# Four feed-forwards on one core: the order of the weight queue's loads, and one addition moved ahead

## The chip, the cores and the metric

The kernel runs on one core of a Trainium2 chip. The metric is the device time of one execution in microseconds, and lower is better. The kernel before takes 2634.15 us, the median of three runs (2631.6 to 2635.01).

## What is computed

Two transformer blocks of two layers each, for 512 tokens of width 1024, all in float32. Each of the four layers ends in a feed-forward, and only these four are touched here:

```
hn = rms_norm(h, gain)                                   # [512, 1024]
h = h + jnp.square(jax.nn.relu(hn @ w1)) @ w2            # w1 [1024, 4096], w2 [4096, 1024]
```

In the second block the norm has a shift and a scale, and the product with `w2` is multiplied by a gate before it is added. The mixers between the feed-forwards (a spatial gate, two chunked recurrences, two attentions) stay as they are.

## The kernel before

Everything is held transposed: 128 features on the partitions, 512 tokens along the free axis. A float32 product is made of three matmuls on values that are cut into a high and a low part (`hi*hi + hi*lo + lo*hi`), so every weight has to be cut before use: ACT writes the high part (`w_hi`), DVE or POOL writes the low part (`w_lo = raw - hi`).

**Loads.** SP issues all weight loads, in one written order (`mlp_stream`, lines 504 to 546). A load of `w1` is a *chunk* (line 509): 128 columns, 512 KB. A load of `w2` is a *half chunk* (line 514): 512 rows by 256 columns, also 512 KB; two of them feed the four products of one step. Each load waits, on SP, for its buffer to be read for the last time. SP handles its list strictly in order, so a load that waits holds back all that stand behind it. In the first three feed-forwards ACT also issues loads of its own (`ada_load_one`, line 563, 512 KB each), up to three per step, for a modulation vector that is summed beside the feed-forward.

**The steps.** A feed-forward begins with six chunks in the plain form and the first four products with `w2` (step 0). Then come the steps `hp` = 1 to 13, and last steps 14 and 15, which have products with `w2` only. Each step 1 to 13 does two things on TensorE (`mlp_tensor`):

- the *pair*: two new chunks of the hidden layer, by seven products P1 to P7 on quarters (Strassen's scheme in Winograd's form, line 1363 and the two after it), instead of eight;
- four products with `w2`, g0 to g3 (line 1398 and the next), for hidden values made earlier; each is added to `h` by DVE (`add`, line 1704).

TensorE's order within a step is P1, P2, g0, P4, P5, P6, g1, P7, g2, P3, g3. P3 adds to a bank that DVE must have read first (`last_quarters`, line 1681).

**The pair's two chunks.** For the step `hp + 1`, the first chunk is needed for its P1 and P2 cuts. The second is needed inside step `hp`: DVE makes the sums S3 and S1 from both chunks (`sums_13(ahead)`, lines 1658 and 1659) right behind `add(hp, 1)`, and ACT makes the high part of P4 from it (line 1489). DVE's list in a step is:

```
mid_low, [ada], low P6, first_quarter, low P7, sum_4 (S4), add g0, [ada], low P3, low P1', [ada], low P2',
add g1, S3', S1', last_quarters, low P4', scaled, add g2, low P5', second_quarter, scaled, S2', mid_low, add g3
```

A prime marks work for the step ahead. The two `scaled` operations are there in the first two feed-forwards only (line 1692), and `[ada]` in the first three. `last_quarters` stands behind S3' and S1' in DVE's list, and TensorE's P3 waits for it.

**What SP waits for.** The second chunk of step `hp + 1` waits for S4 of step `hp` (line 1669). The two half chunks wait for POOL's low cuts of g1 and of g3 of step `hp` (line 654). The first chunk of step `hp + 2` waits for the low cut of P3 of step `hp`. POOL's cut of g3 follows ACT's high part of g3, which stands in ACT's list right behind the high part of P3, which is made from the sum S4.

**The first steps.** In step 0, DVE's list ends: low parts of the turned activations (`t_low`), `add(0, 1)`, `t_low(3)`, `std_rest(5)` (which waits for ACT), `sums_13(1)`, `add(0, 2)`, and so on. TensorE's g0 of step 1 waits for `add(0, 2)`, since it writes the same bank.

Here is how the pair loop of SP reads:

```
for which in range(2):
    ... wait ...
    chunk(...)
for half in range(2):
    sp.wait_ge(*g_cut(i, hp - 1, 2 * half + 1))
    g_chunk(hp, half)
```

Of the kernel before, what the change touches and what calls it, by code (L numbers as in the profile page):

```python
# [102 lines left out]
def program(nc: bass.Bass, dram, out, upto="end"):  # L103
    rows, col, n_tables = vector_rows()
    ctx = ExitStack()
    with ctx:
# [55 lines left out]
        def ready(q, j):  # L162
            return w_ready, 4 * q + j + 1
# [235 lines left out]
        def out_quad(i):  # L399
            return quads[mlp_out[i]] + 1  # L400

        def place(hp, what):

            if hp == 0:
                return 12 + int(what[1])
            if hp >= 14:
                return 160 + 4 * (hp - 14) + int(what[1])
            return 16 + 11 * (hp - 1) + PAIR.index(what)

        def spent(i, n):  # L410
            return ml_spent, N_HALVES * i + n + 1

        def std_cut(i, c, part="lo"):
            return ml_pool, 76 * i + 2 * c + (2 if part == "lo" else 1)

        def g_cut(i, hp, c):
            return ml_pool, 76 * i + 12 + 4 * hp + c + 1
# [9 lines left out]
        def low_cut(i, hp, what):  # L427
            return ml_low, 143 * i + 11 * (hp - 1) + PAIR_LOWS.index(what) + 1
# [19 lines left out]
        def std_acted(i, what, n):  # L448
            return std_act, 12 * i + 2 * n + (2 if what == "hi" else 1)

        def t_at(i, what):
            return t_dve, 20 * i + T_DVE.index(what) + 1

        def t_acted(i, what, n):
            return t_act, (12 * i if i < 2 else 24 + 4 * (i - 2)) + n + 1 + (8 if what == "hi" and i < 2 else 0)
# [8 lines left out]
        def raw_slot(s):  # L464
            return w_raw[:, s, :, :] if s < 4 else raw_extra
# [4 lines left out]
        def pair_load(hp, which):  # L470
            n = 2 * (hp - 1) + which
            s = RING[n % 3]
            return s, n // 3 + (0 if s == 4 else 2)

        def g_load(hp, half):
            if hp < 14:
                return 2 + half, 1 + hp
            return (half, 11) if hp == 14 else (2 + half, 15)

        def land(s):  # L480
            return w_load[s] if s < 4 else extra_load
# [22 lines left out]
        def mlp_stream(sp, i):  # L504

            w1, w2 = mlp_w[i]

            def chunk(s, c):
                sp.dma_start(raw_slot(s), w1[:, c * P:(c + 1) * P].rearrange("(k p) n -> p k n", p=P)).then_inc(land(s), 16)

            def g_chunk(hp, half):
                s, at = g_load(hp, half)[0], hp // 2 * 512
                n = 4 * (hp % 2) + 2 * half
                sp.dma_start(raw_slot(s).rearrange("p (k n) c -> p k (n c)", n=2),
                             w2[at:at + 512, n * P:(n + 2) * P].rearrange("(k p) m -> p k m", p=P)).then_inc(land(s), 16)

            for c in range(4):
                sp.wait_ge(*ready(out_quad(i), c))
                chunk(c, c)
            for which in range(2):  # L520
                sp.wait_ge(*std_cut(i, which))
                chunk(which, 4 + which)
            for half in range(2):
                sp.wait_ge(*std_cut(i, 2 + half))
                g_chunk(0, half)
            for hp in range(1, 14):
                for which in range(2):
                    n = 2 * (hp - 1) + which
                    if n < 2:
                        sp.wait_ge(*std_cut(i, 4 + n))  # L530
                    elif n == 2:
                        sp.wait_ge(*t_at(i, "lo3"))
                    elif n % 2:
                        sp.wait_ge(*low_cut(i, 1 + (n - 3) // 2, "S4"))
                    else:
                        sp.wait_ge(*low_cut(i, 1 + (n - 3) // 2, "P3"))
                    chunk(pair_load(hp, which)[0], 4 * (hp // 2 + 1) + 2 * (hp % 2) + which)
                for half in range(2):
                    sp.wait_ge(*g_cut(i, hp - 1, 2 * half + 1))
                    g_chunk(hp, half)  # L540
            for half in range(2):
                sp.wait_ge(*low_cut(i, 13, "P3" if half else "S4"))
                g_chunk(14, half)
            for half in range(2):
                sp.wait_ge(*g_cut(i, 13, 2 * half + 1))
                g_chunk(15, half)
# [648 lines left out]
        def gate_col(block2_layer, half, n):  # L1195
            if block2_layer is None:
                return 1.0
            c = 48 * block2_layer + 24 * half + 16 + n
            return mod[:, c:c + 1]
# [112 lines left out]
        def g_bank(i, hp, c):  # L1312
            if hp >= 14 and i == 3:
                return ps[0] if c % 2 else ps[3]
            return ps[3 + c % 2]

        def t_pair(p):
            return t_tiles[:, 2 * p:2 * p + 2, :].rearrange("p a t -> p (a t)")
# [274 lines left out]
        def mlp_vector(v, i, layer2, norm_before, next_norm):  # L1593
# [17 lines left out]
            def std_rest(n):  # L1611
                v.wait_ge(*std_acted(i, "hi", n))
                nc.vector.tensor_tensor(m_lo[:, n, :], tt[:, n % 2, :], m_hi[:, n, :].bitcast(F32), ALU.subtract
                                        ).then_inc(std_dve, 1)
# [27 lines left out]
            def t_low(p):  # L1642
                v.wait_ge(*t_acted(i, "hi", p))
                nc.vector.tensor_tensor(xt_lo[:, p, :], t_pair(p), xt_hi[:, p, :].bitcast(F32), ALU.subtract
                                        ).then_inc(t_dve, 1)

            def low(hp, what):
                n = place(hp, what)
                v.wait_ge(*high_cut(i, hp, what))
                nc.vector.tensor_tensor(half_slot(w_lo, n), pair_block(hp, what), half_slot(w_hi, n).bitcast(F32),  # L1650
                                        ALU.subtract).then_inc(ml_low, 1)

            def sums_13(hp):
                a11, _ = quarters_of(hp, 0)
                a21, a22 = quarters_of(hp, 1)
                v.wait_ge(*ml_loaded(i, *pair_load(hp, 0)))
                v.wait_ge(*ml_loaded(i, *pair_load(hp, 1)))
                nc.vector.tensor_tensor(s3_tile, a11, a21, ALU.subtract).then_inc(ml_low, 1)
                nc.vector.tensor_tensor(a21, a21, a22, ALU.add).then_inc(ml_low, 1)
# [41 lines left out]
            def add(hp, c):  # L1701
                n = 4 * (hp % 2) + c
                v.wait_ge(*spent(i, place(hp, f"g{c}")))
                nc.vector.scalar_tensor_tensor(out=h[:, n, :], in0=g_bank(i, hp, c)[:, :], scalar=gate_col(layer2, 1, n),  # L1704
                                               in1=h[:, n, :], op0=ALU.mult, op1=ALU.add).then_inc(ml_added, 1)
# [25 lines left out]
            t_low(2)  # L1731
            add(0, 1)
            t_low(3)
            std_rest(5)
            sums_13(1)
            add(0, 2)
            low(1, "P4")
            low(1, "P5")
            sum_2(1)
# [1936 lines left out]
        def mlp(i, norm_before, next_norm, layer2=None):  # L3676
            return (lambda e: mlp_tensor(e, i, norm_before), lambda e: mlp_scalar(e, i, norm_before, next_norm),
                    lambda e: mlp_vector(e, i, layer2, norm_before, next_norm))
# [175 lines left out]
```

## Time and profile before

| | us |
|---|---|
| Median of three runs | 2634.15 |
| The profiled execution | 2635.26 |
| Its span (first to last instruction) | 2633.5 |
| TensorE busy | 2583.0 (98%) |
| VectorE busy | 1911.9 (73%) |
| ScalarE busy | 1297.3 (49%) |
| GpSimd busy | 1345.1 (51%) |
| Longest group of waits of TensorE in the feed-forwards | 6.6 |

The four feed-forwards lie at about 330 to 676, 1000 to 1330, 1640 to 2005 and 2280 to 2630 us. A busy share is an average over stages. What a reordering is worth in the feed-forwards is read from TensorE's waits there and from how long before its need each load lands.

### The profile page before, as it was taken

Reading aid. Unit: us, or ns where it says so; the run is one execution under the profiler, and the core shown is the slowest. Engines: PE = TensorE matmul, PEld = TensorE weight load, DVE = VectorE, ACT = ScalarE, POOL = GpSimd, SP = SyncE. Lnnn points to the kernel's source line nnn. Section 1 sums busy time; section 2 is a strip of 40 time slices with the busy share of each in tenths; the row PEclk is TensorE's granted clock in tenths of the full one; section 3 lists DMA queues with packets and bytes.
Section 4 is the critical chain, followed back from the end, with each engine's and each line's share of the span. In section 5 each row is a group of like instructions: output and inputs, shape, how many; then the busy total and the mean of one; then the engine's idle time right before and its main releaser. Section 6 shows DMA issues by size and latency. Waiting matters only on the chain.

```text
span 2633.5 us, 39135 instructions
## 1 busy us (share of the span) xinstructions
PE 2583.0 (98%) x14420; PEld 2132.7 (81%) x14420; DVE 1911.9 (73%) x2755; ACT 1297.3 (49%) x2291; POOL 1345.1 (51%) x1720
## 2 busy tenths in 40 slices
PE   9999999999999999999999999999999999999999
PEld 7777788888867778888887887788887666789998
DVE  4766578997677767999854577888875776786664
ACT  4455344444356644444432354455554776455553
POOL 5543543334866665433476866543336655643333
PEclk9999999999999999999999999999999999999999
DMA  5211135554321223555332321255543211233332
GB/s 145 68 48 42 54 123 160 161 160 137 103 72 56 65 64 110 180 166 161 120 120 72 88 65 58 88 170 170 167 138 92 62 59 56 64 97 97 97 97 88
DMA packets 359671, 272.77 MB, mean 104 GB/s; under 512 B 9786, under 2 KB 346052, under 8 KB 359492
## 3 DMA queue, kind: packets, MB, share of 16 engines
q1 hardware_dynamic: 343618, 216.68, 27.8%
q10 hardware_dynamic: 15874, 53.67, 6.1%
q8 instruction: 116, 1.90, 0.3%
q14 instruction: 63, 0.52, 0.1%
HBM read 268.22 MB, written 2.10 MB: 103 GB/s over the span
## 4 chain that ended last, share of the span: by engine, by line
PE 75%; DVE 8%; POOL 7%; issue 5%; ACT 3%; DMA 1%; ACTq 0%; POOLq 0%; DVEq 0%; SPq 0%
PE pair L1401 8%; PE pair L1398 8%; PE pair L1402 8%; POOL w_lo L585 5%; PE ps L1363 4%; PE ps L1366 4%; PE ps L1365 4%; PE pair L1363 3%; PE pair L1366 3%; PE pair L1365 3%; PE ps L675 3%; PE ps L2641 2%; PE ps L677 2%; PE ps L676 2%; POOL w_hi L578 2%
## 5 line engine op out<-in xcount | busy, mean ns | idle before, releaser
L654 POOL TENSOR_TENSOR w_lo<-w_raw,w_hi 128x256 fp32r<-128x256 f32 x512 | 486.5, 972 | 758.4 <-ACT w_hi L1480 758.3
L585 POOL TENSOR_TENSOR w_lo<-w_raw,w_hi 128x256 fp32r<-128x256 f32 x588 | 498.2, 877 | 12.3
L1398 PE MATMUL pair<-m_hi,w_hi 128*128 128x512 f32 x1008 | 394.8, 392 | 4.6 <-DVE h L1704 4.6
L1401 PE MATMUL pair<-m_lo,w_hi 128*128 128x512 f32 x1008 | 395.5, 392 | 0.0
L1402 PE MATMUL pair<-m_hi,w_lo 128*128 128x512 f32 x1008 | 394.4, 391 | 0.0
L591 POOL TENSOR_TENSOR slot_mark<-slot_mark 128x1 f32<-128x1 f32 x168 | 44.2, 263 | 484.3 <-PE ps L677 218.4
L1398 PEld LDWEIGHTS pair<-m_hi,w_hi 128*128 128x128 f32 x1008 | 189.8, 188 | 40.8 <-issue 5.2
L675 PE MATMUL ps<-x_hi,w_hi 128*128 128x512 f32 x528 | 218.1, 413 | 4.5 <-DVE x_lo L1170 2.5
L1402 PEld LDWEIGHTS pair<-m_hi,w_lo 128*128 128x128 f32 x1008 | 189.3, 188 | 40.9
L1489 ACT ACTIVATE w_hi<-w_raw 128x512 fp32r<-128x512 f32 x216 | 135.3, 628 | 176.8 <-DVE w_raw L1669 97.1
L1480 ACT ACTIVATE w_hi<-w_raw 128x512 fp32r<-128x512 f32 x256 | 157.6, 624 | 125.9 <-DMA w_raw<-in_w_mlp_dram 42.5
L1401 PEld LDWEIGHTS pair<-m_lo,w_hi 128*128 128x128 f32 x1008 | 189.7, 188 | 33.5
L677 PE MATMUL ps<-x_hi,w_lo 128*128 128x512 f32 x528 | 206.8, 392 | 0.0
L676 PE MATMUL ps<-x_lo,w_hi 128*128 128x512 f32 x528 | 206.2, 391 | 0.0
L578 POOL TENSOR_SCALAR w_hi<-w_raw 128x512 fp32r<-128x512 f32 x294 | 202.3, 705 | 0.0
L1650 DVE TENSOR_TENSOR w_lo<-w_raw,w_hi 128x512 fp32r<-128x512 f32 x216 | 177.8, 835 | 10.6 <-ACT w_hi L1489 10.6
L1704 DVE SCALAR_TENSOR_TENSOR h<-pair,mod,h 128x512 f32<-128x512 f32 x124 | 93.0, 750 | 121.5 <-PE pair L1402 121.4
L2641 PE MATMUL ps<-x_hi,w_hi 128*128 128x512 f32 x336 | 139.6, 415 | 1.5
L1495 ACT ACTIVATE rb<-ps 128x256 f32<-128x256 f32 x156 | 59.8, 383 | 155.5 <-PE ps L1366 155.4
L2643 PE MATMUL ps<-x_hi,w_lo 128*128 128x512 f32 x336 | 131.7, 392 | 0.0
L2642 PE MATMUL ps<-x_lo,w_hi 128*128 128x512 f32 x336 | 131.6, 392 | 0.0
L1704 DVE SCALAR_TENSOR_TENSOR h<-pair,h 128x512 f32<-128x512 f32 x128 | 87.8, 686 | 60.3 <-PE pair L1402 60.0
(552 smaller groups left out, 7056.6 us busy)
## 6 DMA issues: line engine op xcount, KB each, us to landing
w_raw<-in_w_mlp_dram SPq DMA_DIRECT2D x112, 512.0 KB, 5.3
w_raw<-in_mlp_w_dram SPq DMA_DIRECT2D x112, 512.0 KB, 5.2
arena<-in_ada_w_dram ACTq DMA_DIRECT2D x96, 512.0 KB, 4.6
w_raw<-in_w_in_ab_dram SPq DMA_DIRECT2D x28, 512.0 KB, 3.8
w_raw<-in_w_qkv_o_dram SPq DMA_DIRECT2D x24, 512.0 KB, 3.7
w_raw<-in_w_qkv_dram SPq DMA_DIRECT2D x24, 512.0 KB, 3.8
w_raw<-in_w_in_e_dram SPq DMA_DIRECT2D x23, 512.0 KB, 4.1
arena<-in_w_mlp_dram SPq DMA_DIRECT2D x16, 512.0 KB, 5.5
```

The source lines that it names most:

```text
L578: last = nc.gpsimd.tensor_scalar(w_hi[:, j, k, :], w_raw[:, j, k, :], 1.0, 1.0, ALU.mult, ALU.mult)
L585: last = nc.gpsimd.tensor_tensor(w_lo[:, j, k, :], w_raw[:, j, k, :], w_hi[:, j, k, :].bitcast(F32), ALU.subtract)
L654: last = nc.gpsimd.tensor_tensor(half_slot(w_lo, n)[:, k, :], g_half(hp, c)[:, k, :], half_slot(w_hi, n)[:, k, :].bitcast(F32), ALU.subtract)
L675: nc.tensor.matmul(bank[:, :], w_hi[:, j, k, :], hi[:, k, :], start=(k == 0), stop=False)
L676: nc.tensor.matmul(bank[:, :], w_hi[:, j, k, :], lo[:, k, :], start=False, stop=False)
L677: last = nc.tensor.matmul(bank[:, :], w_lo[:, j, k, :], hi[:, k, :], start=False, stop=(k == ND - 1))
L1363: nc.tensor.matmul(out, hi[:, t, :], b_hi[:, t, :], start=(start and t == 0), stop=False, skip_group_check=True)
L1365: nc.tensor.matmul(out, hi[:, t, :], b_lo[:, t, :], start=False, stop=False, skip_group_check=True)
L1398: first = nc.tensor.matmul(bank[:, :], hi[:, t, :], m_hi[:, m, :], start=(t == 0), stop=False)
L1401: nc.tensor.matmul(bank[:, :], hi[:, t, :], m_lo[:, m, :], start=False, stop=False)
L1402: last = nc.tensor.matmul(bank[:, :], lo[:, t, :], m_hi[:, m, :], start=False, stop=(t == 2))
L2641: nc.tensor.matmul(ps[0][:, :], w_hi[:, j, k, :], hi[:, k, :], start=(k == 0), stop=False)
```

## The change

Two edits. In SP's list, for the steps 2 to 13, both half chunks now stand between the pair's first and second chunk. Step 1 is as before. In DVE's list of step 0, `add(0, 2)` goes ahead of `std_rest(5)` and `sums_13(1)`. No instruction is added or removed, no wait is changed, and buffers are the same.

```diff
@@ mlp_stream
                     chunk(pair_load(hp, which)[0], 4 * (hp // 2 + 1) + 2 * (hp % 2) + which)
-                for half in range(2):
-                    sp.wait_ge(*g_cut(i, hp - 1, 2 * half + 1))
-                    g_chunk(hp, half)
+                    if which == (1 if hp == 1 else 0):
+                        for half in range(2):
+                            sp.wait_ge(*g_cut(i, hp - 1, 2 * half + 1))
+                            g_chunk(hp, half)
@@ mlp_vector
             add(0, 1)
             t_low(3)
+            add(0, 2)
             std_rest(5)
             sums_13(1)
-            add(0, 2)
             low(1, "P4")
```

In SP's list of the first feed-forward, the loads of steps 1 to 4 stood like this before (a row with `128x8x128` is a chunk, one with `128x4x256` a half chunk, `x2` means two in a row; the third buffer for chunks is called `arena`):

```order
L509 DMA w_raw<-in_w_mlp_dram 128x8x128 x2
L514 DMA w_raw<-in_w_mlp_dram 128x4x256 x2
L509 DMA arena<-in_w_mlp_dram 128x8x128
L509 DMA w_raw<-in_w_mlp_dram 128x8x128
L514 DMA w_raw<-in_w_mlp_dram 128x4x256 x2
L509 DMA w_raw<-in_w_mlp_dram 128x8x128
L509 DMA arena<-in_w_mlp_dram 128x8x128
L514 DMA w_raw<-in_w_mlp_dram 128x4x256 x2
```

and now:

```order
L509 DMA w_raw<-in_w_mlp_dram 128x8x128 x2
L514 DMA w_raw<-in_w_mlp_dram 128x4x256 x2
L509 DMA arena<-in_w_mlp_dram 128x8x128
L514 DMA w_raw<-in_w_mlp_dram 128x4x256 x2
L509 DMA w_raw<-in_w_mlp_dram 128x8x128 x2
L514 DMA w_raw<-in_w_mlp_dram 128x4x256 x2
L509 DMA arena<-in_w_mlp_dram 128x8x128
L509 DMA w_raw<-in_w_mlp_dram 128x8x128
```

The second chunk of each step from 2 on now stands behind the step's two half chunks and right ahead of the next step's first chunk.

In DVE's list of the first feed-forward, the end of step 0 before, from `add(0, 1)` on:

```order
L1704 SCALAR_TENSOR_TENSOR h<-pair,h 128x512
L1644 TENSOR_TENSOR xt_lo<-arena,xt_hi 128x1024
L1613 TENSOR_TENSOR m_lo<-tt,m_hi 128x512
L1658 TENSOR_TENSOR tt<-w_raw 128x512
L1659 TENSOR_TENSOR w_raw<-w_raw 128x4x128
L1704 SCALAR_TENSOR_TENSOR h<-pair,h 128x512
L1650 TENSOR_TENSOR w_lo<-w_raw,w_hi 128x512 x2
```

and now (lines behind the first edit count one higher):

```order
L1705 SCALAR_TENSOR_TENSOR h<-pair,h 128x512
L1645 TENSOR_TENSOR xt_lo<-arena,xt_hi 128x1024
L1705 SCALAR_TENSOR_TENSOR h<-pair,h 128x512
L1614 TENSOR_TENSOR m_lo<-tt,m_hi 128x512
L1659 TENSOR_TENSOR tt<-w_raw 128x512
L1660 TENSOR_TENSOR w_raw<-w_raw 128x4x128
L1651 TENSOR_TENSOR w_lo<-w_raw,w_hi 128x512 x2
```

The second addition moved three instructions ahead: it stands before the low part of the last plain chunk and the first pair's two sums.

## Rows read from the trace of the kernel before

**Rows 1.** The page, busy time of each engine over the span.
```profile
PE 2583.0 (98%) x14420; PEld 2132.7 (81%) x14420; DVE 1911.9 (73%) x2755; ACT 1297.3 (49%) x2291; POOL 1345.1 (51%) x1720
```

**Rows 2.** TensorE's waits: engine, tile, line, for whom: us in total, times, longest.
```profile
PE pair L1363 <- DVE sq L1681: 6.6, 4, 3.0
PE pair L1398 <- DVE h L1704: 4.6, 6, 1.3
```

**Rows 3.** SP's issues in step 5, first feed-forward: start, us taken, line.
```profile
471.72 0.37 SPq L514 DMA_DIRECT2D w_raw<-in_w_mlp_dram  x1
472.13 0.51 SPq L509 DMA_DIRECT2D w_raw<-in_w_mlp_dram  x1
```

**Rows 4.** Loads issued at 352.7, 468.6, 470.7, 472.1, 380.8 us: KB, us to landing.
```profile
w_raw<-in_w_mlp_dram SPq DMA_DIRECT2D x1, 512.0 KB, 3.6
...
w_raw<-in_w_mlp_dram SPq DMA_DIRECT2D x1, 512.0 KB, 5.5
...
arena<-in_ada_w_dram ACTq DMA_DIRECT2D x1, 512.0 KB, 4.6
...
w_raw<-in_w_mlp_dram SPq DMA_DIRECT2D x1, 512.0 KB, 6.5
...
w_raw<-in_w_mlp_dram SPq DMA_DIRECT2D x1, 512.0 KB, 7.9
```

**Rows 5.** DVE in steps 5 and 6, first feed-forward: start, us, line.
```profile
467.48 0.68 DVE L1669 TENSOR_TENSOR w_raw<-arena,w_raw 128x512 f32<-128x512 f32 x1
...
475.48 0.68 DVE L1658 TENSOR_TENSOR tt<-w_raw,arena 128x512 f32<-128x512 f32 x1
476.08 1.23 DVE L1659 TENSOR_TENSOR arena<-arena 128x512 f32<-128x512 f32 x1
477.23 0.68 DVE L1681 TENSOR_TENSOR sq<-pair,rb 128x512 f32<-128x512 f32 x1
...
488.58 0.68 DVE L1669 TENSOR_TENSOR arena<-w_raw,arena 128x512 f32<-128x512 f32 x1
```

**Rows 6.** P3's first matmul in step 5, feed-forwards one, three and four.
```profile
478.88 0.28 PE L1363 MATMUL pair<-x_hi,w_hi 128*128 128x256 f32 x1
...
1807.90 0.28 PE L1363 MATMUL pair<-x_hi,w_hi 128*128 128x256 f32 x1
...
2429.90 0.28 PE L1363 MATMUL pair<-x_hi,w_hi 128*128 128x256 f32 x1
```

**Rows 7.** SP issuing the later half chunk, step 5, feed-forwards three and four.
```profile
1800.53 0.37 SPq L514 DMA_DIRECT2D w_raw<-in_mlp_w_dram  x1
...
2421.47 0.37 SPq L514 DMA_DIRECT2D w_raw<-in_mlp_w_dram  x1
```

**Rows 8.** P3's first matmul in steps 1 and 12, feed-forwards one and two.
```profile
390.99 0.52 PE L1363 MATMUL pair<-x_hi,w_hi 128*128 128x256 f32 x1 [3.02 <-DVE sq L1681]
...
628.06 0.28 PE L1363 MATMUL pair<-x_hi,w_hi 128*128 128x256 f32 x1
...
1056.50 0.39 PE L1363 MATMUL pair<-x_hi,w_hi 128*128 128x256 f32 x1 [1.30 <-DVE sq L1681]
...
1290.93 0.28 PE L1363 MATMUL pair<-x_hi,w_hi 128*128 128x256 f32 x1
```

**Rows 9.** SP issuing the later half chunk in step 1, feed-forwards one and two.
```profile
383.95 0.37 SPq L514 DMA_DIRECT2D w_raw<-in_w_mlp_dram  x1
...
1051.17 0.37 SPq L514 DMA_DIRECT2D w_raw<-in_w_mlp_dram  x1
```

**Rows 10.** Busy time, instructions, granted clock, DMA share, GB/s behind the longest wait.
```profile
391.00:394.50 3.50, 3.50 (x14) 3.31 (x15) 2.91 (x6) 1.81 (x3) 0.00 (x0) 0.51 0.35 129
```

**Rows 11.** ACT in step 1 of the first feed-forward.
```profile
388.73 0.63 ACT L1480 ACTIVATE w_hi<-w_raw 128x512 fp32r<-128x512 f32 x1 [5.76 <-DMA w_raw<-in_w_mlp_dram]
```

**Rows 12.** `add(0, 2)` and the g0 that waits for it, second feed-forward.
```profile
1040.10 0.68 DVE L1704 SCALAR_TENSOR_TENSOR h<-pair,h 128x512 f32<-128x512 f32 x1
...
1040.93 0.47 PE L1398 MATMUL pair<-m_hi,w_hi 128*128 128x512 f32 x1 [0.89 <-DVE h L1704]
```

## The prediction

> **What bounds the kernel now.** I read the page first: TensorE is busy for 98% of the span, every other engine for 73% or less [rows 1]. So there is almost nothing to win, and the question is what lies idle in the feed-forwards and how close the other waits are to showing. The waits of TensorE say what is idle. Those that this change can touch are 6.6 us in four waits at P3, which waits for DVE's `last_quarters`, and 4.6 us in six waits of products with `w2` for an addition to `h` [rows 2]. That is 0.4% of the time. The longest is 3.0 us in step 1 of the first feed-forward, and behind it the granted clock was 0.51, its lower level of 1.2 GHz, for most of 3.5 us [rows 8, 10]. ACT had waited there 5.76 us for the step's early half chunk, which took 7.9 us to land behind the second chunk and two loads of ACT [rows 11, 4]. This is what the new order would help.
>
> Then I read the order of time of SP, DVE and TensorE inside one later step, since steps 2 to 13 repeat with a period of 21.10 us (S4 starts at 467.48 and at 488.58) [rows 5]. There TensorE waits for nothing. What counts is the slack. In step 5 of the first feed-forward, S3' starts at 475.48, S1' at 476.08, `last_quarters` runs from 477.23 to 477.91, and P3 starts at 478.88 [rows 5, 6]. P3 could have borne 0.97 us less the handover, which is 0.06 us.
>
> **The queue edit.** It moves no work, it moves one landing. Until now SP issued the second chunk of the next step as soon as S4 ended, at 468.16 (467.48 + 0.68). Now it stands behind the later half chunk, which waits for POOL's cut of g3 and was issued at 471.72; the next entry of the list followed 0.41 us later, at 472.13 [rows 3]. So the second chunk goes out at 472.13 instead of about 468.2, 3.9 us later.
>
> *How long it then takes to land (D).* No row shows this chunk in this place. The nearest are: 3.6 us for a load with nothing in flight; 5.5 us for one issued 0.41 us behind another; 6.5 us for the one at 472.13, which had the older loads and one of ACT's in front (ACT's own took 4.6) [rows 4]. The earlier half chunk will be out of the way by then, so I take 5.5, from the row with the same neighbour in front, and keep 3.6 and 6.5 as ends; 7.9 is the worst row.
>
> The Trainium skill (DMA: Bandwidth & Descriptors, section Anatomy of one DMA) gives 2.0 us plus the bytes over 436 GB/s for one transfer, though for the gpsimd path. By that page 512 KB would be an estimated 3.2 us alone and 4.0 us behind another one. No row here is so short.
>
> *What hangs on it.* S3' and S1' read the second chunk, and `last_quarters` stands behind them. S3' start to the end of `last_quarters` is 2.43 us now; S1' took 1.23 us where S3', of the same shape, took 0.68, and POOL's cut of g0' beside it now comes earlier (its half chunk is no longer late), so I take 2.43 − 0.55 = 1.9. From the later half chunk's issue to P3 it is then 0.41 + D + 1.9 + 0.1 for two handovers, **7.9 us with D = 5.5**. The room is 478.88 − 471.72 = 7.16 us in the first two feed-forwards, 1807.90 − 1800.53 = 7.37 in the third, 2429.90 − 2421.47 = 8.43 in the fourth [rows 3, 6, 7]. So P3 comes 0.75 us late, 0.5 us late, and in time. ACT's P4' and the cut behind it wait for the same landing, but need only about 1.0 us before `last_quarters`, less than S3' and S1', so they are hidden.
>
> *The circle.* Lateness feeds itself. Late S3' shifts all of DVE's list behind it up to S4 of the next step; S4 releases ACT's P3 and g3 and POOL's cut, that releases the later half chunk, and that the next second chunk. From S3' (475.48) to the end of S4 (489.26) are 13.78 us, with nearly no gap in the first two feed-forwards; less 0.55 for S1' and some 0.1 of gaps, 13.1. From the end of S4 (468.16) to the half chunk's issue (471.72), 3.56. With 0.41, D = 5.5 and 0.05 of handover the circle is **22.6 us**. A step took (1290.93 − 1056.50) / 11 = 21.31 us on the mean [rows 8]. DVE had idle time before; waiting for the load uses it up. So the steps of the first two feed-forwards get 1.3 us longer each. In the third there are no two `scaled` (0.6 us each) and the circle is near 21.8, so P3's own lateness counts, 0.5 to 0.75: I take 0.6. In the fourth DVE has no `[ada]` either, and the circle is hidden.
>
> **The addition.** `add(0, 2)` has 0.6 us of DVE (0.68 with overlapped ends), and stands in front of S3' and S1' of step 1 no more. TensorE's g0 had waited 0.89 us for it in the second feed-forward [rows 12]. `std_rest(5)` waits for ACT anyway, so the addition is free ahead of it. TensorE's own gain at g0 is given back, since P3 of step 1 was late in three feed-forwards; what stays is DVE's 0.6 us. Once per feed-forward, all queues behind it 0.6 us earlier.
>
> **Sum, against the profiled execution (2635.3 us).**
>
> - *First steps.* First feed-forward: 383.95 − 0.6 + 7.9 = 391.25 against 390.99, +0.3 [rows 8, 9]. Second: 1051.17 − 0.6 + 7.9 = 1058.5 against 1056.50, +2.0. Third: as the second, +2.0, and since the whole wait is then over 3 us, the lower clock behind it as in the first: 3.5 us at 0.51 cost half, +1.8 [rows 10]. In the second DVE's circle hides that. Fourth: +0.5, P3 had no wait there before.
> - *Later steps, eleven from P3 of step 1 to P3 of step 12.* First: 11 × 22.6 = 248.6 against 628.06 − 390.99 = 237.1, +11.5. Second: 248.6 − 234.4 = +14.2. Third: 11 × 0.6 = +6.6. Fourth: 0.
>
> Together 11.8 + 16.2 + 10.4 + 0.5 = **+38.9 us**, so 2674.2; the median of the runs shown was 1.1 us under the profiled execution, so I predict **2673 us**, 1.5% slower. What a measurement of this kernel can tell from no change is about 0.2%, 5.3 us.
>
> **Rivals.**
>
> - *Hidden.* If the second chunk lands within 4.4 us of its issue in the first two feed-forwards (22.6 − 21.31 = 1.3 less than 5.5 would be 4.2, P3's own room gives 4.75), nothing shows in the later steps. For it: ACT's load falls behind it (ACT issues the third one after P4', which now waits) and the half chunks leave its way. Against: 5.5 us in a row with just one load in front. The first steps then give −0.8 in the first, about +0.8 in each of the next two: near 2635. By the page's estimate of 4.0 us this is what would come out. Chance 0.08.
> - *Faster.* The place is step 1 of the first feed-forward: with the half chunk no longer late and a landing of 3.6 us, P3 starts at 389.3, 1.7 us earlier; a wait as short as the 1.3 us of the second feed-forward left the clock up, so the 1.8 us go too, and about 1.1 us of the other three waits of [rows 2], first line. With the addition's 0.6 us twice that is 5.8 us, about 2628. It decides from D = 3.7 downwards. Chance 0.07.
> - *Heavier.* The three loads now go out in one burst with ACT's beside them. With D = 6.5 the circle is 23.6: 11 more us in each of the first three and P3 0.5 us late in each step of the fourth: +38.9 + 33 + 5.5 + 4 = +81, about 2716. For it: 6.5 and 7.9 in rows 4. Chance of more than 2712: 0.10.
> - That the edit does nothing can be left out: eleven issues per feed-forward are moved for certain, and the later half chunk's wait is a real one.
>
> **Chances.** The forecast's mechanism, with D from 4.7 to 6.4, gets 0.75 and spans 2642 (at 4.7: circle 21.8, +5 and +7 in the first two feed-forwards, nothing in the later steps of the others) to 2712. The range 2642 to 2712 leaves out the hidden and faster cases and the worst of the heavier. Faster by over 0.2%: 0.07; within: 0.08; slower: 0.85.
>
> **What would show it.** In the profile after: a second chunk issued about 0.4 us behind the later half chunk; DVE idle 2 us before S3' (L1659 there), with a DMA as the releaser; TensorE's wait at P3 for `last_quarters` in nearly every step, some 30 of them over 0.5 us; steps of about 22.6 us in the first two feed-forwards, 21.9 in the third, 21.1 in the fourth; g0 of step 1 with no wait for an addition. Wrong would be: a landing under 4.7 us with no wait at P3 (hidden), steps of equal length in all four feed-forwards (then no circle through DVE), or the fourth as slow as the others (then it is the burst, not DVE's list).

## The result, and the profile after

The changed kernel takes **2754.6 us** (median of 4 runs, 2752.4 to 2762.5) against 2632.9 us before (median of 4 runs on the same chip). The ratio is 1.0466, with an interval of 1.0452 to 1.0480: 122 us slower. Predicted were 2673 us and at most 2712.

The page of the kernel after, busy times. The third figure of an engine's group is its number of instructions.

```profile
PE 2618.8 (95%) x14420; PEld 2152.8 (78%) x14420; DVE 1910.0 (69%) x2755; ACT 1286.1 (47%) x2291; POOL 1358.9 (49%) x1720
```

The work is the same, but TensorE is busy for 35.8 us more than in [rows 1], its weight loads for 20 and GpSimd for 14. A large part of TensorE's is work done at the lower clock: in run 6 below, with 56 us less of that clock, it is busy for 24 us less. The span grew by 119 us, from 2633.5 to 2752.6. The summary of its chain of waits says who holds the end:

```profile
PE 58%; DVE 15%; DMA 9%; POOL 7%; issue 6%; ACT 4%; ACTq 0%; DVEq 0%; POOLq 0%
```

The same line of the kernel before, in which DMA has 1% and TensorE 75%:

```profile
PE 75%; DVE 8%; POOL 7%; issue 5%; ACT 3%; DMA 1%; ACTq 0%; POOLq 0%; DVEq 0%; SPq 0%
```

TensorE's waits after, which answer to [rows 2]:

```profile
PE pair L1364 <- DVE sq L1682: 90.5, 37, 6.6
PE pair L1399 <- DVE h L1705: 2.4, 4, 1.0
```

P3 waits 37 times for `last_quarters`, 90.5 us in all, where there were four waits and 6.6 us. All but two of the 37 are in the first three feed-forwards. The addition's waits went from 4.6 to 2.4 us. DVE in turn waits for the second chunk before S3' (three of its four lines with a DMA as the releaser; with the fourth, 18.7 us, they are 48 waits of 3.0 us on the mean):

```profile
DVE tt L1659 <- DMA w_raw<-in_w_mlp_dram: 62.3, 16, 5.3
DVE tt L1659 <- DMA w_raw<-in_mlp_w_dram: 33.8, 16, 4.2
DVE tt L1659 <- DMA arena<-in_w_mlp_dram: 27.2, 8, 4.8
```

One turn of the circle, in order of time, steps 4 and 5 of the second feed-forward. DVE first (start, us taken, line, and in brackets how long it was idle and what ended that):

```profile
1171.73 0.69 DVE L1659 TENSOR_TENSOR tt<-arena,w_raw 128x512 f32<-128x512 f32 x1 [3.78 <-DMA w_raw<-in_w_mlp_dram]
1172.34 0.69 DVE L1660 TENSOR_TENSOR w_raw<-w_raw 128x512 f32<-128x512 f32 x1
1172.94 0.69 DVE L1682 TENSOR_TENSOR sq<-pair,rb 128x512 f32<-128x512 f32 x1
...
1184.00 0.68 DVE L1670 TENSOR_TENSOR w_raw<-arena,w_raw 128x512 f32<-128x512 f32 x1
...
1196.52 0.69 DVE L1659 TENSOR_TENSOR tt<-w_raw,arena 128x512 f32<-128x512 f32 x1 [4.82 <-DMA arena<-in_w_mlp_dram]
```

SP's queue in the same stretch, and what it says of the landing of the load at 1188.65 (KB, us from issue to landing):

```profile
1188.24 0.37 SPq L514 DMA_DIRECT2D w_raw<-in_w_mlp_dram  x1
1188.65 0.51 SPq L509 DMA_DIRECT2D arena<-in_w_mlp_dram  x1
...
arena<-in_w_mlp_dram SPq DMA_DIRECT2D x1, 512.0 KB, 7.8
```

S3' starts at 1171.73, S4 ends at 1184.68 (12.95 us), the later half chunk is issued at 1188.24 (3.56), the second chunk 0.41 behind it, it lands 7.8 us later, and the next S3' starts at 1196.52: 24.8 us for a step that took 21.3. S3' start to the end of `last_quarters` is 1173.63 − 1171.73 = 1.90 us, and P3 follows at 1173.68:

```profile
1173.68 0.38 PE L1364 MATMUL pair<-x_hi,w_hi 128*128 128x256 f32 x1 [2.25 <-DVE sq L1682]
```

P3's first matmul after, in steps 1 and 12 of the four feed-forwards in turn (the first and second pairs answer to [rows 8]):

```profile
395.09 0.58 PE L1364 MATMUL pair<-x_hi,w_hi 128*128 128x256 f32 x1 [5.86 <-DVE sq L1682]
...
666.41 0.39 PE L1364 MATMUL pair<-x_hi,w_hi 128*128 128x256 f32 x1 [0.62 <-DVE sq L1682]
...
1098.70 0.58 PE L1364 MATMUL pair<-x_hi,w_hi 128*128 128x256 f32 x1 [6.03 <-DVE sq L1682]
...
1369.31 0.39 PE L1364 MATMUL pair<-x_hi,w_hi 128*128 128x256 f32 x1 [0.57 <-DVE sq L1682]
...
1805.66 0.58 PE L1364 MATMUL pair<-x_hi,w_hi 128*128 128x256 f32 x1 [6.55 <-DVE sq L1682]
...
2073.90 0.37 PE L1364 MATMUL pair<-x_hi,w_hi 128*128 128x256 f32 x1
...
2463.03 0.39 PE L1364 MATMUL pair<-x_hi,w_hi 128*128 128x256 f32 x1
...
2696.66 0.28 PE L1364 MATMUL pair<-x_hi,w_hi 128*128 128x256 f32 x1
```

Over eleven steps that is 271.3, 270.6, 268.2 and 233.6 us, where before it was 237.1, 234.4, 234.4 (1722.7 to 1957.1) and 232.0 (2345.5 to 2577.5). So **the later steps cost +34.2, +36.2, +33.8 and +1.6 us, 106 of the 119**, and a step is 24.7, 24.6, 24.4 and 21.2 us long. The first steps (from P1's first matmul to P3's) cost +2.7, +3.6, +4.2 and +0.3; the remaining 2.5 us are elsewhere.

And the landing time in place. The burst of step 4, first feed-forward: a load of ACT at 460.12, the later half chunk at 461.03, the second chunk at 461.44, the next first chunk at 461.99 (KB, us to landing, in this order). Then a half chunk and a second chunk at 2518.0 and 2518.4 in the fourth feed-forward, which has no load of ACT. Last, the second chunk of step 13 in the first feed-forward, issued at 659.40, which has none beside it either:

```profile
arena<-in_ada_w_dram ACTq DMA_DIRECT2D x1, 512.0 KB, 4.1
...
w_raw<-in_w_mlp_dram SPq DMA_DIRECT2D x1, 512.0 KB, 6.4
...
w_raw<-in_w_mlp_dram SPq DMA_DIRECT2D x1, 512.0 KB, 7.6
...
w_raw<-in_w_mlp_dram SPq DMA_DIRECT2D x1, 512.0 KB, 8.6
...
w_raw<-in_mlp_w_dram SPq DMA_DIRECT2D x1, 512.0 KB, 3.7
...
w_raw<-in_mlp_w_dram SPq DMA_DIRECT2D x1, 512.0 KB, 5.1
...
w_raw<-in_w_mlp_dram SPq DMA_DIRECT2D x1, 512.0 KB, 5.0
```

The means in the trace after (us; D is the second chunk's issue to landing), with those before in brackets. The first two columns are over the loads of steps 3 to 13, the last three over those of steps 2 to 13:

| feed-forward | D | later half chunk to landing | S3' start to S4 end | S4 end to half chunk's issue | that issue to S3' |
|---|---|---|---|---|---|
| 1 | 6.9 (4.4) | 5.6 (6.0) | 13.4 (14.1) | 3.8 (3.7) | 7.5 (3.7) |
| 2 | 6.9 (4.4) | 5.6 (5.6) | 13.3 (13.8) | 3.8 (3.7) | 7.5 (3.6) |
| 3 | 7.1 (4.5) | 5.5 (5.6) | 12.8 (13.3) | 4.0 (4.0) | 7.7 (3.9) |
| 4 | 5.4 (4.4) | 3.8 (4.9) | 12.4 (13.1) | 2.9 (2.9) | 5.8 (5.0) |

In the first three rows the last three columns add up to the measured step within 0.1 us (24.7, 24.6, 24.4): the circle closes. In the fourth row they make 21.1 and little waits. In the first three feed-forwards D depends on ACT: in the 33 steps 2 to 12 a load of ACT was issued 0.6 to 1.8 us ahead of the later half chunk, and D is 7.2 us on the mean; in the three steps 13 there is none, and D is 4.9. The granted clock was at about half (1.2 GHz) for 6.8 us of the span before and for 75.4 us, in 18 stretches, of the span after.

### The profile page after: what moved, and what is told of

Same layout as the page of the kernel before. It is cut to its first block, busy times and chain, and to the rows that moved or that the text cites. A ratio compares the mean times of both kernels' runs of the same rounds, so it can differ in the third digit from the quotient of the medians.

```text
span 2752.6 us, 39135 instructions
## 1 busy us (share of the span) xinstructions
PE 2618.8 (95%) x14420; PEld 2152.8 (78%) x14420; DVE 1910.0 (69%) x2755; ACT 1286.1 (47%) x2291; POOL 1358.9 (49%) x1720
## 4 chain that ended last, share of the span: by engine, by line
PE 58%; DVE 15%; DMA 9%; POOL 7%; issue 6%; ACT 4%; ACTq 0%; DVEq 0%; POOLq 0%
PE pair L1399 5%; PE pair L1402 5%; PE pair L1403 5%; POOL w_lo L586 5%; DMA w_raw<-in_w_mlp_dram 4%; DVE w_lo L1651 3%; PE ps L676 2%; DMA w_raw<-in_mlp_w_dram 2%; PE ps L2642 2%; PE ps L678 2%; PE ps L677 2%; PE ps L1364 2%; POOL w_hi L579 2%; PE pair L1364 2%; PE ps L1367 2%
## 5 line engine op out<-in xcount | busy, mean ns | idle before, releaser
L655 POOL TENSOR_TENSOR w_lo<-w_raw,w_hi 128x256 fp32r<-128x256 f32 x512 | 499.4, 998 | 862.3 <-ACT w_hi L1481 862.2
L586 POOL TENSOR_TENSOR w_lo<-w_raw,w_hi 128x256 fp32r<-128x256 f32 x588 | 497.9, 877 | 12.3
L1399 PE MATMUL pair<-m_hi,w_hi 128*128 128x512 f32 x1008 | 401.1, 398 | 2.4 <-DVE h L1705 2.4
L1364 PE MATMUL pair<-x_hi,w_hi 128*128 128x256 f32 x208 | 68.8, 331 | 90.6 <-DVE sq L1682 90.5
L1490 ACT ACTIVATE w_hi<-arena 128x512 fp32r<-128x512 f32 x96 | 60.0, 628 | 160.3 <-DVE arena L1670 49.0
```

Of the source, the lines that this page charges most:

```text
L586: last = nc.gpsimd.tensor_tensor(w_lo[:, j, k, :], w_raw[:, j, k, :], w_hi[:, j, k, :].bitcast(F32), ALU.subtract)
L655: last = nc.gpsimd.tensor_tensor(half_slot(w_lo, n)[:, k, :], g_half(hp, c)[:, k, :], half_slot(w_hi, n)[:, k, :].bitcast(F32), ALU.subtract)
L1399: first = nc.tensor.matmul(bank[:, :], hi[:, t, :], m_hi[:, m, :], start=(t == 0), stop=False)
L1490: nc.scalar.activation(half_slot(w_hi, n), pair_block(hp, what), ACT.Copy).then_inc(ml_hi, 1)
```

## The experiments

My theory after the result: the mechanism is the predicted one (late second chunk, circle through DVE's list and SP's queue), and D was mis-sized. Rivals for the size: the lower clock behind P3's waits, the bandwidth taken by the first chunk behind, or something in the addition. The kernel before, beside which they ran on the same chip, had medians of 2632.2 us (1 to 4), 2634.0 (5, 6, 7 and 11) and 2632.2 (8, 9, 10 and 12); the ratios are to these runs. They are formed from all runs and differ from the quotient of two medians by up to 0.0007.

**1, 2. Each part alone.** The first is the kernel before with the addition's line moved; the second is the changed kernel with the line put back, so only SP's order is changed:

```diff
             t_low(3)
+            add(0, 2)
             std_rest(5)
             sums_13(1)
-            add(0, 2)
```
(the second kernel has this piece reversed, against the changed kernel).

> Only the addition to h is moved ahead; SP's list is as before. If the whole slowdown is the queue's (my theory), this is 0.5 to 3 us faster than before: TensorE's wait of 0.9 us at g0 of step 1 in the second and of 1.3 us in the third feed-forward goes, and part of it is given back at P3. If the moved addition carries part of the slowdown, it is more than 5 us slower than before.

Measured: 2631.2 us, ratio 0.9996 (0.9987 to 1.0005). That lies in the range I gave, but it is not to be told from nothing. The trace shows what it does, TensorE's waits of this kernel:

```profile
PE pair L1363 <- DVE sq L1681: 5.6, 3, 2.1
PE pair L1398 <- DVE h L1704: 2.4, 4, 1.0
```

About 1.0 us less at P3 and 2.2 less at the additions, in a kernel whose runs differ by more.

> Only SP's list is changed. Theory: all of the +122 us, 2754 to 2757 us. Rival (the two edits hurt only together): under 2740 us.

Measured: 2758.9 us, 1.0481 (1.0465 to 1.0497), 2 us above the range of my theory and far from the rival's. **The queue's order carries all of the loss.**

**3. One half chunk between the chunks.** SP's order in a step is first chunk, early half chunk, second chunk, later half chunk; the addition stays ahead.

```diff
-                    if which == (1 if hp == 1 else 0):
-                        for half in range(2):
+                    if hp == 1 and which == 1 or hp > 1:
+                        for half in range(2) if hp == 1 else [which]:
                             sp.wait_ge(*g_cut(i, hp - 1, 2 * half + 1))
                             g_chunk(hp, half)
```

> SP's list of steps 2 to 13 is first chunk, early half chunk, second chunk, later half chunk, and the addition is ahead. The second chunk no longer stands behind POOL's cut of g3, so by my theory it goes out right behind S4 again, about 5.4 us into a step, lands near 9.5, and the slowdown is gone: 2624 to 2632 us, with the wait of 3 us at P3 in step 1 of the first feed-forward shorter, since ACT has its half chunk early. Rival (an early half chunk in itself disturbs the loads, or the split of the pair does): over 2660 us.

Measured: 2630.5 us, 0.9997 (0.9988 to 1.0006), as expected. The second chunk is out early again and D is 4.1 us. So it is the later half chunk, which waits for POOL's cut of g3, that the second chunk must not stand behind. The early one ahead of it costs nothing, and brings nothing that shows either: P3 still waits in three of the first steps.

```profile
PE pair L1364 <- DVE sq L1682: 5.9, 3, 2.3
```

**4. Take P3 off the late chunk, keep the circle.** The changed kernel with `last_quarters` ahead of `sums_13` in DVE's list, and ACT's snap P7 ahead of the cut P4'. P3 then needs nothing of the second chunk, but S4 still stands behind S3'.

```diff
                 add(hp, 1)
+                last_quarters(hp)
                 if hp < 13:
                     sums_13(ahead)
-                last_quarters(hp)
@@ on ACT
                 g_high(ahead, 0)
+                snap(hp, "P7", snap_v)
                 if hp < 13:
                     high(ahead, "P4")
                 ada_ahead(2)
-                snap(hp, "P7", snap_v)
```

> The changed kernel, with DVE's last_quarters ahead of S3' and S1' and ACT's snapshot of P7 ahead of the high part of P4', so that P3 does not wait for the second chunk. If the slowdown is P3's wait alone (the order of DVE's list), 2625 to 2645 us. If it is the circle (S3' late, DVE's list late up to S4, the later half chunk and the next second chunk late), the circle with the measured landing of 7 us is 12.5 + 3.6 + 0.4 + 7.0 + 0.1 = 23.6 us against 21.3, and the first three feed-forwards keep steps of 23 to 24 us: 2690 to 2720 us.

Measured: 2688.7 us, 1.0215 (1.0199 to 1.0231), at the lower end of what the circle would make (2690 to 2720) and far from the 2625 to 2645 of the other case. P3's own waits shrink to 13 us, the half clock to 3.4 us, and yet the kernel is 56 us slower than before. TensorE now waits for low parts that DVE makes late:

```profile
PE pair L1399 <- DVE m_lo L1699: 23.7, 29, 2.3
PE pair L1364 <- DVE sq L1682: 13.0, 22, 1.1
PE ps L1364 <- DVE w_lo L1651: 11.7, 9, 2.1
```

Steps (from P3 of step 1 to P3 of step 12, by eleven, as above) are 23.7, 23.9, 22.3 and 21.1 us. In the first feed-forward S3' to S4 is 12.3, then 3.7 and 7.4: 23.4, which again adds up to nearly the whole step, with D still at 6.8. **The circle is there with TensorE's wait at P3 taken out of it.** It also shows how much of a turn was TensorE's. S3' to S4's end fell from 13.4 to 12.3 us in the first feed-forward and from 12.8 to 10.8 in the third. Of either, 0.6 us is `last_quarters` itself, which stood in this stretch and now runs ahead of S3', while DVE waits for the load. The rest is mostly waits for TensorE: in this stretch DVE was idle for 0.5 and 1.6 us a turn in the changed kernel, each time for a product, and in run 4 for nothing in the first feed-forward and for 0.9 us, for ACT, in the third. Ahead of S4 in DVE's list stand `second_quarter`, which waits for P3, and `add(hp, 3)`, which waits for g3 behind it. P3's wait, the lower clock and this 0.6 us together are worth 66 us, and the other 56 are there without them.

**5. As late, but first in the burst.** One line holds the second chunk until POOL's cut of g3; it then goes out ahead of the later half chunk (the order is that of 3).

```diff
                         sp.wait_ge(*low_cut(i, 1 + (n - 3) // 2, "S4"))
+                        sp.wait_ge(*g_cut(i, hp - 1, 3))
```

> The order of the run before (early half chunk, second chunk, later half chunk), but the second chunk also waits for POOL's cut of g3, so it goes out as late as in the changed kernel, only in the later half chunk's place, 0.41 us earlier and first in the burst. Circle theory: it lands in the 5.6 us that the later half chunk took there, so the circle is 13.2 + 3.8 + 5.7 = 22.7 us in the first two feed-forwards, P3 late by 0.3 us in the third, nothing in the fourth: 2655 to 2675 us, some 85 us below the changed kernel for 1.7 us of earlier landing. Rival (cost follows from the late issue, whatever the landing): 2730 us or more.

Measured: 2671.8 us, 1.0150 (1.0133 to 1.0167), in the range of the circle theory and far from the rival's. D is 5.8, 5.8, 5.5 and 4.4 us. So with nothing of SP's queue right in front it is still 5.5 to 5.8 in the first three feed-forwards, and in the fourth, where ACT loads nothing, 4.4. The circle in the first: 12.9 + 4.2 + 5.5 = 22.6, with steps of 22.6 and 22.5 in the first two. One place nearer to the front, and 0.41 us less of issue, are worth 83 us.

**6. ACT's load out of the burst.** In the changed kernel ACT issues the second of its three loads of a step behind P4', with the third, instead of 0.6 to 1.8 us ahead of the later half chunk.

```diff
                     high(ahead, "P2")
-                ada_ahead(1)
                 snap(hp, "P6", snap_q)
                 g_high(ahead, 0)
                 if hp < 13:
                     high(ahead, "P4")
+                ada_ahead(1)
                 ada_ahead(2)
```

> The changed kernel, with ACT's second load of a step issued behind the high part of P4', so that none of ACT's loads is in flight when the later half chunk and the second chunk go out. If ACT's load is why the second chunk takes 6.9 to 7.1 us in the first three feed-forwards and 5.4 in the fourth, it takes 5.3 to 5.8 now, and the circle is 1.3 us shorter over 33 steps: 2700 to 2715 us. If the burst of SP's own three loads is the reason, the landing and the time stay: 2745 us or more.

Measured: **2672.2 us**, 1.0146 (1.0130 to 1.0162). That is 82 us less than the changed kernel, and 28 us below the range that I expected here. D came down as the theory said, but a step got 2.1 to 2.3 us shorter and not the 1.3 expected, over 36 steps and not 33. The time is nearly the one predicted for the changed kernel, since its steps are nearly those forecast there; in part that is luck, D being 0.3 us under the 5.5 taken and the wait for POOL's cut 0.2 over. D is 5.2, 5.2, 5.3 and 5.4 us: all four feed-forwards alike. One second chunk of the first feed-forward (issued at 473.71 us; KB, us to landing):

```profile
arena<-in_w_mlp_dram SPq DMA_DIRECT2D x1, 512.0 KB, 5.4
```

TensorE's waits at P3 fall to a third, with hardly fewer of them, and the half clock to 20 us:

```profile
PE pair L1364 <- DVE sq L1682: 32.8, 31, 4.5
```

The steps are 22.6, 22.5, 22.0 and 21.3. Over twelve steps and the first three feed-forwards that is (2.1 + 2.1 + 2.3) × 12 = 78 us less than in the changed kernel, so the steps hold nearly all of the 82. The later half chunk, next behind ACT's load before, took 3.7 us instead of 5.6.

**7. The first chunk held back.** In the changed kernel SP waits for the second chunk to have landed before it issues the next first chunk, so nothing is behind it in its queue.

```diff
                         sp.wait_ge(*low_cut(i, 1 + (n - 3) // 2, "P3"))
+                        sp.wait_ge(*ml_loaded(i, *pair_load(hp - 1, 1)))
```

> The changed kernel, with the next step's first chunk held on SP until the second chunk has landed, so that only two of SP's loads are in the burst. If the load behind it takes bandwidth from the second chunk, that one lands 0.5 to 1.5 us sooner and the time is 2700 to 2735 us. If what is behind in SP's own queue does not matter: within 6 us of the changed kernel.

Measured: 2730.8 us, 1.0370 (1.0354 to 1.0387), 24 us less than the changed kernel. The time lies in the range of the first case, but the landing that was to bring it does not: D hardly moved, 6.8, 6.9, 6.7 and 5.1 us against 6.9, 6.9, 7.1 and 5.4. That is 0.1, 0.1 and 0.4 us in twelve steps each, 7 us in all; the half clock was 61 us instead of 75. The span of the profiled execution was 2739 us, only 13 us under the changed kernel's, and its waits at P3 were 85.3 us in 37 times, close to the 90.5 above. **What stands behind the second chunk in its queue is not what makes D long.** Which of the small gains make up the 24 us stays open.

**8. Filler for the clock.** Six matmuls more in each of steps 1 to 12 of the first three feed-forwards, from TensorE, into a bank that nobody reads, ahead of P3's wait and behind one for ACT's cut of P3; what the kernel computes is unchanged.

```diff
                 g_product(hp, 2)
+                if i < 3 and hp < 13:
+                    pe.wait_ge(*low_cut(i, hp, "P3"))
+                    for _ in range(6):
+                        nc.tensor.matmul(ps[5][:, :], half_slot(w_hi, place(hp, "P3"))[:, 0, :], x_hi[:, 0, :],
+                                         start=True, stop=True)
                 pe.wait_ge(*pair_out(i, hp, "C2"))
```

> The changed kernel, and in steps 1 to 12 of the first three feed-forwards six more matmuls of 512 columns on TensorE ahead of P3's wait, into a bank that nobody reads (1.4 us of work inside a wait of 2.5 us on the mean; they change no result). They add 216 matmuls and shorten the idle time, so the lower clock should stay away. If the lower clock costs what 68 us at half speed lose (34 us), 2715 to 2725 us. If most of it is hidden behind DVE's circle in the first two feed-forwards, 2730 to 2745 us. If it costs nothing, 2750 to 2760 us, or more by what the filler delays in steps with a shorter wait.

Measured: 2746.9 us, 1.0440 (1.0420 to 1.0459). The time lies between two of my cases. The half clock fell from 75 to 40 us, and P3's waits from 90.5 to 50.4 us:

```profile
PE pair L1364 <- DVE sq L1687: 50.4, 31, 5.1
```

Yet the kernel gained only 8 us (7 by the ratios, whose intervals leave about 1 to 13 open), and the steps are still 24.8, 24.3 and 24.0 us. D was 7.3, 7.0 and 7.0 us, so 0.4 longer in the first feed-forward, which takes some 5 us of the gain away. **The lower clock is not the larger part of the loss.** A reason that fits, though no run shows it apart: TensorE runs slow while the circle, which doesn't wait for it most of the time, sets the end. By this run 36 us less at half clock are worth 8 us, or 13 with those 5; all 75 us would then be 17 to 27, a rough estimate. Run 6 says the same in another way: of its 82 us, 36 × 1.7 = 61 are D, which leaves 21 for the clock (20 us at half in it instead of 75) and the rest. A part of the half clock remained, and what the filler itself delayed is not told apart from what it gained, so the clock's share stays an estimate.

**9 to 12. Is there a version that beats both?** 9 is the kernel before with the lists of 4; 10 adds the addition to it; 11 is 3 with the lists of 4, that is one half chunk between, the addition and the lists; 12 is 11 with ACT's edit of 6. Their diffs are those above.

> The kernel before with last_quarters ahead of S3' and S1' and ACT's snapshot of P7 ahead of P4', nothing else. P3's waits in step 1 (6.6 us and 1.8 us of lower clock) were due to these two lists: 3 to 8 us faster than before. If the early half chunk and the addition are needed for it: within 2 us of before.

> The run with all edits, but with the queue of before: the addition ahead and the two lists changed. If the half chunk between the pair's chunks gave nothing, this is as fast as the version with all of them, 2625 to 2628 us. If it gave part of the 7 us: 2628 to 2631 us.

> A version to beat both: one half chunk between the pair's chunks, the addition ahead, last_quarters ahead of S3' and S1', and ACT's snapshot of P7 ahead of P4'. P3's waits in step 1 (5.9 us in three feed-forwards) go, no step gets longer: 2621 to 2628 us. Rival (the waits only move to another product of step 1): 2628 to 2633 us.

> The version with all edits and ACT's second load of a step issued behind P4' as well. No wait of the later steps is left for it to shorten, so the same within 2 us: 2625 to 2629 us. If contention with ACT's load still costs in step 1, 1 to 3 us faster.

| | us | ratio to before | interval |
|---|---|---|---|
| 9, the lists | 2630.3 | 0.9986 | 0.9977 to 0.9995 |
| 10, the lists and the addition | 2627.4 | 0.9979 | 0.9970 to 0.9988 |
| 11, one half chunk between as well | 2626.9 | 0.9974 | 0.9964 to 0.9984 |
| 12, ACT's load later as well | 2625.7 | 0.9979 | 0.9969 to 0.9989 |

All four beat the kernel before, by 0.1 to 0.3%. 9 is at the lower edge of what I expected: 1.9 us faster by the medians, 3.7 by the ratio. 10, 11 and 12 came out inside their ranges. The one remaining wait at P3 in 9, of the first feed-forward, is not made by S3' but by the early half chunk, for which ACT waits 6.15 us; the chunk took 8.3 us to land:

```profile
PE pair L1363 <- DVE sq L1681: 2.9, 1, 2.9
```

In 10 the same line is down to nothing. But SP's list is the same there, and the half chunk landed in 5.1 us; so this is the landing of one execution and not the addition's doing:

```profile
PE pair L1363 <- DVE sq L1681: 0.5, 2, 0.3
```

10 to 12 can't be told apart: their intervals overlap, so neither the half chunk's place nor ACT's load shows on top of the lists and the addition. The interval of 9 overlaps theirs as well, so the addition on top of the lists is not shown to gain either; that the lists do is.

## Why the prediction was right in direction and wrong in size

**Right: what the edit does.** The second chunk goes out 0.41 us behind the later half chunk. S3' to the end of `last_quarters` is 1.90 us, as taken. DVE waits before S3' for a DMA (3.0 us on the mean, 2 were forecast), and P3 for DVE in 37 steps, 36 of them over 0.5 us (some 30 were forecast). The fourth feed-forward has hardly a wait (+1.6 us where 0 stood), and the waits for an addition fell from 4.6 to 2.4 us. The addition alone, 0.6 us per feed-forward in my sum, lies within what run 1 can tell. The sign and the place of the loss were as said.

**Wrong: "How long it then takes to land (D)", 5.5 us.** Measured 6.9, 6.9 and 7.1 in the first three feed-forwards, and 5.4 only in the fourth. I took the row with the same neighbour in SP's queue in front, 5.5, and set aside the 6.5 of [rows 4], which "had the older loads and one of ACT's in front". But ACT's load is there in each step from 2 to 12: it is released by ACT's list, which the change leaves as it was, and it goes out 0.6 to 1.8 us ahead of the later half chunk. In step 13, where it is absent, D is 4.9 us in all three. I did put ACT's third load behind the second chunk, and forgot the second one. Run 6 settles it, by taking just this load away: D 5.2 us, 2672 us. Run 7 leaves the load behind at most 0.4 us of it. My end of 7.9 us for D ("the worst row") would have been the better end of the range than 6.5; the range stopped at D = 6.4. The row of 7.9 was read wrongly too: of the "two loads of ACT" that the chunk was said to land behind, the trace of the kernel before has one landing at 380.7 us, just ahead of the chunk's issue at 380.8, and the other issued 1.4 us after it.

**The circle's other terms**, first and second feed-forward: 13.1 was 13.4, 3.56 was 3.8, 0.41 and 0.05 were about 0.5 together. Of the 2.05 us by which a turn is longer than my 22.6, D is 1.4, and these nearly the rest. One reason for the 13.1 is that I took 0.55 us off each turn for a faster S1', from one row of 1.23 us; S1' took that long in 16 of 52 steps before. The range's lower end has a slip that bears on nothing: with a circle of 21.8 the formula gives +2.7 and +5.4, not "+5 and +7".

**Wrong as a consequence: the third feed-forward, "I take 0.6".** I had its circle at 21.8, just 0.5 over a step, so that P3's own lateness would decide. It is 12.8 + 4.0 + 7.7 = 24.4, and the step 24.4: +33.8 us where I had +6.6. D gives 1.6 of the 2.6. Most of the other 1.0 is my subtraction of two `scaled`, 1.2 us: S3' to S4 is only 0.6 shorter than in the others. Run 4 shows why: with P3 freed it drops by 2.0 us there, 1.4 of them beyond the moved `last_quarters`, and DVE's waits for TensorE in it go from 1.6 us a turn to nothing. That stretch is not DVE's work end to end, but holds waits for TensorE, which itself waits at P3. So P3's lateness and DVE's circle are one loop in the third, not two cases of which the longer counts.

**The lower clock.** Forecast for one step, 1.8 us; it was 75 us in 18 stretches. Behind the two kinds of wait, with engine busy times, clock, DMA share and GB/s (the stretch behind the wait of 5.86 us, then one behind a wait of 2.25 us):

```profile
395.00:398.40 3.40, 3.31 (x14) 3.21 (x15) 2.78 (x6) 1.64 (x4) 0.00 (x0) 0.50 0.27 111
1173.60:1177.00 3.40, 3.32 (x20) 3.03 (x21) 3.37 (x7) 1.88 (x4) 0.24 (x1) 1.00 0.25 100
```

It would have been a large term if each stretch had counted; by runs 6 and 8 it is an estimated 17 to 27 us of 122. That and the first steps (+10.8 us, forecast +6.6 with the clock) are the small terms. In the first step of the first feed-forward D was even 7.7 us (issued at 385.40, landed by 393.1).

**The sum again.** With D = 6.9 in place of 5.5 my own formula gives a circle of 24.0: 11 × 24.0 − 237.1 = +26.9 and 11 × 24.0 − 234.4 = +29.6; for the third 11 × (21.8 + 1.4) − 234.4 = +20.8. With 10.8 for the first steps that is +88. The rest, about 31, are the other terms of the circle (0.65 us in 22 steps, 14 us), the third's loop (1.2 in 11 steps, 13 us) and 4 us elsewhere and in the fourth. The lower clock is no term of its own in this sum; its part lies in the steps.

**The rivals.** *Hidden* and *faster* needed D under 4.7 and 3.7 us; a landing as short as 3.7 was seen in the changed kernel for half chunks alone. The faster case's mechanism, the early half chunk no longer late, was tried without the cost in run 3, and is worth nothing that shows there. *Heavier* was the right one, for its reason (ACT's load beside the burst), and its 2716 was still 39 us short. It had a chance of 0.10, and should have been the forecast. The estimate by the page of the Trainium skill (DMA: Bandwidth & Descriptors, Anatomy of one DMA), 4.0 us behind another load, is not what the traces show: 5.4 us on the mean in the fourth feed-forward, 4.9 at the least, where only the later half chunk is in front, and that load took 3.7 to 3.8.

## What to carry to other kernels

A load's landing time is read from a row at the same place in the burst, with the loads of the other engines counted: here one load of 512 KB from another queue, 0.6 to 1.8 us ahead, added 1.5 to 2.3 us. Where a late load delays a serial list whose later entries release the next load, a wait isn't hidden or paid once: the full turn is added up (list, release, issue, landing) and compared with the period, and from there on each microsecond is paid in each step, 36 times here. A load that is needed first is not put behind one whose release comes later; in a queue that issues in order it takes over that one's lateness, and its bandwidth.

## What the runs showed of the hardware that was not expected

- **Two engines' queues share one pace.** A later half chunk of 512 KB took 3.7 us with no load of ACT ahead of it (fourth feed-forward, steps 13 and run 6), and 5.5 us on the mean of a feed-forward with one ahead; a second chunk behind it 4.9 to 5.4, and 6.9 to 7.1. The load that was behind it in the queue made at most 0.4 us of difference (run 7). From 485 to 494 us of the changed kernel's trace the DMA engines moved 232 GB/s on the mean, and about 300 in the middle of the burst.
- **Lower clock that costs little.** 36 us less of it brought 8 us (run 8), where another chain sets the end of a step. And of two waits of the same kind one of 5.86 us had 0.50 behind it, and one of 2.25 us 1.00.
- **The same DVE sum at two speeds.** S3' and S1' both took 0.69 us (1171.73 and 1172.34) where S1' had taken 1.23 in [rows 5]. Before, S1' took 1.2 us in the 16 of 52 steps in which a cut of POOL was running when it started, and 0.7 in the other 36; after, no cut runs there, and it took 0.7 in all 52. S4 took 1.2 us in the 42 steps after with a cut of POOL running at its start, and 0.7 in the other 10.
